# Attention in steps of head pairs: the division of the probabilities moved from VectorE to GpSimd

## What is computed

```python
m = max(scores over all keys, and the sink logit if there is one)
e = exp(scores - m)
p = e / (e.sum(-1) + exp(sink - m))      # the sink's term only where there is a sink
o = p @ v
```

## Time and profile before

| | us |
|---|---|
| median of three runs | 2708.22 |
| lowest and highest | 2704.76, 2711.07 |
| the profiled execution's own time | 2708.02 |
| its span | 2706.2 |
| TensorE busy | 2602.3 |
| VectorE busy | 1407.0 |
| ScalarE busy | 568.7 |
| GpSimd busy | 544.9 |

### The profile page before, as it was taken

How to read it: one execution, slowest core, us unless ns; L and a number is a source line. 1 busy time by engine, 2 the same in 40 slices (tenths; PEclk the granted TensorE clock), 3 DMA queues, 4 the chain that set the end, 5 groups by cost and what they waited for, 6 DMA issues and landing times.

```text
span 2706.2 us, 37981 instructions
## 1 busy us (share of the span) xinstructions
PE 2602.3 (96%) x15358; PEld 1817.8 (67%) x15358; DVE 1407.0 (52%) x2740; ACT 568.7 (21%) x1142; POOL 544.9 (20%) x420
## 2 busy tenths in 40 slices
PE   8999999999999999999999999999999999999998
PEld 4347568888865655789974444788888746555554
DVE  2766376466757677642655653675555427310111
ACT  1216121100033333321022032100000216201110
POOL 0000034344400000038850000354354000000000
PEclk9999999999999999999999999999999999999998
DMA  9540035554333423445436410455543300499995
GB/s 349 199 167 32 31 132 202 179 187 171 114 86 101 116 74 101 141 155 173 156 125 208 142 63 32 151 184 179 172 140 132 111 26 1 195 417 412 416 405 228
DMA packets 222415, 446.67 MB, mean 165 GB/s; under 512 B 18874, under 2 KB 124153, under 8 KB 219163
## 3 DMA queue, kind: packets, MB, share of 16 engines
q1 hardware_dynamic: 180896, 329.78, 34.0%
q10 hardware_dynamic: 41338, 114.40, 12.5%
HBM read 443.01 MB, written 1.13 MB: 164 GB/s over the span
## 4 chain that ended last, share of the span: by engine, by line
PE 88%; DVE 6%; ACT 2%; DMA 1%; issue 1%; POOL 0%; SPq 0%; ACTq 0%; DVEq 0%; POOLq 0%
PE bank L1138 35%; PE bank L966 24%; PE bank L3021 5%; PE bank L990 4%; PE bank L3040 3%; PE bank L982 2%; PE bank_pair L3021 2%; PE bank L559 1%; DMA arena<-in_moe_w 1%; PE bank L2095 1%; PE bank L3057 1%; PE bank_pair L3040 1%; PE bank L2088 1%; PE bank L2994 1%; PE bank L2308 1%
## 5 line engine op out<-in xcount | busy, mean ns | idle before, releaser
L1138 PE MATMUL bank<-arena,slot 128*128 128x256 f32 (+1 forms) x3704 | 677.0, 343 | 6.3 <-DVE arena L1118 2.9
L1138 PEld LDWEIGHTS bank<-arena,slot 128*128 128x128 f32 x3704 | 605.0, 191 | 70.6 <-issue 8.1
L1151 POOL TENSOR_TENSOR slot<-slot 128x512 f32<-128x512 f32 (+3 forms) x208 | 269.2, 1294 | 1556.8 <-PE bank L1138 705.1
L966 PE MATMUL bank<-uT,slot 128*128 128x512 f32 (+2 forms) x1312 | 485.1, 525 | 3.0 <-ACT arena L2128 3.0
L966 PEld LDWEIGHTS bank<-uT,slot 128*128 128x128 f32 (+1 forms) x1312 | 246.8, 190 | 217.3 <-issue 205.0
L1138 PE MATMUL bank<-uT,slot 128*128 128x256 f32 (+1 forms) x1728 | 335.9, 351 | 8.6 <-ACT uT L731 8.3
L1138 PEld LDWEIGHTS bank<-uT,slot 128*128 128x128 f32 x1728 | 291.3, 192 | 46.8 <-ACT uT L731 12.0
L1152 POOL TENSOR_TENSOR slot<-slot 128x512 f32<-128x512 f32 (+3 forms) x208 | 286.5, 1378 | 0.0
L966 PE MATMUL bank<-arena,slot 128*128 128x256 f32 (+1 forms) x576 | 184.5, 483 | 3.4 <-DVE arena L1817 2.3
L966 PEld LDWEIGHTS bank<-arena,slot 128*128 128x128 f32 x576 | 111.4, 194 | 75.0 <-issue 66.3
L700 DVE SCALAR_TENSOR_TENSOR arena<-arena 128x1024 f32<-128x1024 f32 x95 | 122.3, 1297 | 18.2 <-issue 14.5
(11 more groups left out here) (459 smaller groups left out, 2990.3 us busy)
## 6 DMA issues: line engine op xcount, KB each, us to landing
slot<-in_ffn_w SPq DMA_DIRECT2D x42, 2048.0 KB, 8.9
arena<-in_ada_wt ACTq DMA_DIRECT2D x100, 512.0 KB, 3.6
slot<-in_moe_w SPq DMA_DIRECT2D x62, 704.0 KB, 16.5
arena<-in_moe_w SPq DMA_DIRECT2D x52, 704.0 KB, 17.5
rstd<-in_ada_wt ACTq DMA_DIRECT2D x48, 512.0 KB, 3.6
slot<-in_moe_w SPq DMA_DIRECT2D x11, 2048.0 KB, 19.1
slot<-in_ssd_w_in SPq DMA_DIRECT2D x32, 512.0 KB, 6.9
uT<-in_ada_wt ACTq DMA_DIRECT2D x28, 512.0 KB, 3.6
```

The lines of the kernel that those rows point to most:

```text
L966: ins = pe.matmul(bank[0:m, 0:t1 - t0], w[:, k, c0:c0 + m], x[:, k, t0:t1], start=(k == 0), stop=(k == kt - 1))
L1138: ins = pe.matmul(bank[:, u * n:u * n + n], a[:, k, u * P:u * P + P], x[:, k, :], start=(k == 0), stop=(k == self.h - 1))
L1151: pool.tensor_tensor(out[:, :, 0:c], x[:, :, 0:c], y[:, :, 0:c], op)
```

## The change

`Attention` becomes a pooled stage. VectorE computes the reciprocals, raises `shares` and goes on without waiting for them; GpSimd waits for `shares`, does the two multiplications of the unit in place, and raises `divided` after each. TensorE's turn waits for `divided` instead of `pn` where the unit is not a `sub` one.

```diff
         class Attention(Stage):
             all_banks = True
+            pooled = True
...
             def turn(self, pe, B, u, a):
 
-                pe.wait_ge(*S("pn").taken("pe"))
+                pe.wait_ge(*S("pn" if self.units[u]["sub"] else "divided").taken("pe"))
...
                 dve.wait_ge(*S("pr").taken("dve"))
                 if it["sink"] is not None:
                     dve_link(ch, dve.tensor_tensor(den, den, es, ALU.add))
-                dve_link(ch, dve.reciprocal(rc, den))
-                for a in range(2):
-                    s = self.score(u, a)
-                    dve.tensor_scalar(s, s, rc[:, a:a + 1], None, ALU.mult).then_inc(*S("pn").given())
+                dve.reciprocal(rc, den).then_inc(*S("shares").given())
+
+            def pool(self, pool, B, ch):
+
+                for u, it in enumerate(self.units):
+                    if not it["sub"]:
+                        rc = self.stats(u)[4]
+                        pool.wait_ge(*S("shares").taken("pool"))
+                        for a in range(2):
+                            s = self.score(u, a)
+                            pool.tensor_scalar(s, s, rc[:, a:a + 1], None, ALU.mult).then_inc(*S("divided").given())
```

More of the change, by code:

```diff
@@ L285, in build @@
         for n in ("loads", "first_loads", "logit_loads", "mod_ready", "squares", "rstd_used", "root", "normed",
-                  "a_rows", "sg_exp", "gla_d", "gla_e", "gla_q", "gla_sm",                   "gla_s", "gla_sp", "gla_y", "cum_full", "cum_free", "gla_el",                   "conv", "feat", "rows_kept", "seg", "segx", "xw", "st", "padded", "gate_summed", "gated", "lw", "lwx", "ecx",                   "nm", "pr", "pn", "hid", "stored", "dti", "dtx",
+                  "a_rows", "sg_exp", "gla_d", "gla_e", "gla_q", "gla_sm",                   "gla_s", "gla_sp", "gla_y", "cum_full", "cum_free", "gla_el",                   "conv", "feat", "rows_kept", "seg", "segx", "xw", "st", "padded", "gate_summed", "gated", "lw", "lwx", "ecx",                   "nm", "pr", "pn", "shares", "divided", "hid", "stored", "dti", "dtx",
                   "free_a", "bias_loads", "rope_in", "head", "convd", "ada_rows", "ada_cols", "ada_copied", "moe_loads", "da_done", "ready", "lam", "picked", "gate_cols", "overflow_known", "moe_rl", "guest_rows", "token_sums", "weight_sums", "guest_read", "late_const", "hid_done", "tiles_done", "ctx_in", "expert_rows", "ranked", "hid_turned"):
```

## The result

The changed kernel took **2728.86 us** (median of four runs, 2727.95 to 2730.05); the kernel before, run beside it, 2709.38. The ratio is 1.0074, with a 95% interval of 1.0058 to 1.0090: slower by over 0.2%. The forecast was 2713.0 with a range of 2706 to 2722. The measured time lies outside both, and the likeliest case, no change that a measurement can tell, is not what came.

The account below looks back on a forecast made before the run. VectorE was taken to bound both attention patterns by a small margin, TensorE right behind. Even stage +3.1, odd stage +1.2 and TensorE's clock +0.5 made +4.8 us on 2708.22: forecast 2713.0, range 2706 to 2722.

Parts of the forecast that it names:

- the price: GpSimd's time for one division, scaled from its tensor_tensor: 0.90 us for 512 columns, 0.50 for 256.
- the forecast's loops: Repeating chains through two divisions P: even group 9.84 + 2P plus 0.15 port wait, two odd units 5.19 + 2P.
- the dear rival: GpSimd's division as slow as its two-input operation, 1.23 us: near +10, 2718; at 1.5 us, 2724; chance 0.22.
- the forecast's own formulas: Start, loops and end summed per stage: even +0.5, +2.0, +0.6, together +3.1 us; odd +0.5, +0.7, together +1.2.
- three whole loops: Even stage: sixteen units counted as three group loops at about +0.67 us each, +2.0 us.
- the end proper: Even stage's end: the last 256 step's two divisions in the open, 0.22 + 1.00 + 0.10 against 0.7, +0.6 us.
- The start: Each stage's first turn comes 1.22 us behind the reciprocal where it came 0.74 behind: +0.5 us.
- The end lies behind eight sub units and costs nothing: Odd stage's end: no added time, covered by the sub units; without that cover 0.6 us more.
- VectorE bounded by a small margin: Both stages: VectorE sets the pace by 1.4 us of an even group and 0.27 of an odd unit, TensorE right behind.
- the forecast case: Both stages: division of 0.8 to 1.05 us, total +3 to +7 us, 2711 to 2715; chance 0.42.
- The signs named for "wrong": Pitch under 11.1, division far from 0.9, negated maxima of 0.5 us or more, or mid-stage granted clock below 1.00.
- ports or clock: Rival: negated maxima meeting divisions at the shared port, +10 us, or TensorE at half speed inside the pattern, +25; chance 0.10.

Follow-up runs that it names:

- e11_short_both: Against the kernel before: GpSimd divides both heads of the 256-key units only, with the two-input form; 2707.18 us, ratio 0.9995.
- e3_two_inputs: The changed kernel with GpSimd's multiplication by the reciprocal broadcast as a second tensor instead of a scalar; 2712.12 us, ratio 1.0013 to the kernel before.
- e8_no_port: The changed kernel with the negated maximum of units without a sink made in two one-column operations; 2727.34 us, ratio 1.0071 to the kernel before.
- e6_one_head_two_inputs: The changed kernel with VectorE dividing head 0 and GpSimd only head 1, in the two-input form; 2713.98 us, ratio 1.0017 to the kernel before.
- e5_one_head: The changed kernel with VectorE dividing head 0 and GpSimd only head 1, in the scalar form; 2713.23 us, ratio 1.0015 to the kernel before.
- e9_own_first: e6_one_head_two_inputs with GpSimd waiting for VectorE's own division instead of the reciprocal; 2710.24 us, ratio 1.0005 to the kernel before.

## Why the prediction was wrong

**The step that failed is the price.** "I scale the column part by two thirds (0.73 + 0.13 = 0.87) and take 0.90 us." The runs show 1.54 and 0.91, which is 0.28 fixed and 2.5 ns a column: dearer, not cheaper, than the engine's tensor_tensor with two real inputs. One stream less is not one third less. With a broadcast second input the same multiplication takes 1.00, near the 0.90 taken, and with it the forecast's loops hold to 0.1 us. Why the form with a scalar is dearer is open: the pointer is 0.08 of it, the neighbourhood of VectorE none that shows, and the rest was not separated. The Trainium skill ("GPSIMD Engine Reference", "4.1 Engine selection") calls one-input operations of this engine roughly line-rate; this trace differs with 2.5 ns a column for float32 in place, and the measurement decides.

**The bound from above was drawn too low.** The forecast called 1.23 "the only row there is" for the dear rival, noted that more was not excluded and worked out 2724 at 1.5, but let the range end at 2722, and gave all of the dear case 0.22. The nearest row was of another form of instruction; it was read as a ceiling because a simpler operation seemed to have to be cheaper.

**With the true price** the forecast's own formulas give, in the even stage, +1.1 at the start, three times 9.84 + 3.08 + 0.15 - 11.07 = 2.0, and +1.4 at the end: +8.5 of the 13.1 measured. The difference goes both ways:
- *The second loop.* A single pair of divisions was followed. Where GpSimd is dearer than 1.1 us the two 512-key units stand in its queue together: 13.92 a group in place of 13.07, some 0.85 each time.
- *The last group.* "The sixteen units hold three whole loops" left out the fourth group. From unit 12's reciprocal to unit 15's it is 8.75 where it was 5.97: another +2.8. Behind that it is 4.27 where it was 3.14, so the end proper is +1.1, near the +1.4 of the formula. Unit 15's own divisions don't stand in GpSimd's queue. They wait for their reciprocal, and by the chain that waits for ScalarE, which may fill unit 13's buffer only after its late turn (line 2535 is its copy, line 2547 stands behind its exponentials).
- *The start.* Its +1.1 did not come on top. TensorE waits 4.79 for the first division where it waited 3.55, but the first group grew by 2.8, like the third.
- *The clock*, 0.7 us: the second group took 14.60 where the third took 13.92, and it holds the stretch at 0.72. Eight outputs take 0.66 us at the full 2.4 GHz and 1.12 in that stretch. In that group the chain is that of the forecast's loop, two divisions and TensorE's work, stretched by the clock past the 13.92 of the other.

The chain at the end of the even stage, parts left out:

```profile
1645.04 0.60 ACT uT L2535
1645.63 0.95 ACTq L2547
...
1646.61 0.18 DVE small L2593
...
1646.87 1.83 POOL uT L2603 x2
```

In the odd stage the pattern is right: 5.19 + 2 x 1.54 = 8.27 for two units against 8.36 measured, +5.3 over seven units. The start's +1.1 did not come on top here either: the first reciprocal stands 5.5 behind the stage's first matmul in both. "The end lies behind eight sub units and costs nothing" is refuted: 1.85 us came there. From the last unit's reciprocal to the first differential one's it is now 4.21 where it was 2.68, since TensorE's next scores stand behind the turn that waits for the last pair, and VectorE's maxima behind those scores.

```profile
2275.26 0.17 DVE L2593 RECIPROCAL small<-small 128x2 f32<-128x2 f32 x1
2279.47 0.15 DVE L2611 RECIPROCAL small<-small 128x1 f32<-128x1 f32 x1
```

**What was right, and how far.** VectorE bounded by a small margin: taking 4.7 us off VectorE without putting anything on the path bought nothing measurable (e11_short_both). But it was not a queue of VectorE alone. Of the 11.07 us of a group in the kernel before, the way from the turn at 1608.47 to the scores at 1613.92 is TensorE's, and the rest VectorE's; so the division stood in a loop before as well, at VectorE's price. With some 1.3 us less on VectorE in each group (e11_short_both) the group got 0.23 shorter, and the chain of that kernel goes through TensorE for most of it. VectorE's busy time in the even stage fell to 30.0, where 27 was said; the held maxima are 1.6 of the difference (16 of them take 4.3 us, and 2.7 at 0.17). e3_two_inputs is near the forecast case as it was priced: +3.6 us on the medians (ratio 1.0013), where +4.8 was worked out for 0.90. By the stages it is +3.9 and +2.5 (3.4 at a like clock), where the formulas with 1.00 and 0.57 give +4.1 and +1.9. TensorE's waits are released by GpSimd. The signs named for "wrong" were those that came: a division far from 0.9, negated maxima of 0.56 us and a granted clock below 1.00 in the middle of the even stage. Of the rival "ports or clock" the price was wrong: the port's part is hidden (e8_no_port), the clock's is 0.7 in the one group where it can be told, and not 25.

## What to carry to other kernels

Before an operation is moved to an engine that nothing here has seen do it, measure that operation in that form; the price of its neighbour is neither a floor nor a ceiling, and a rewriting of the same arithmetic can change it by a third. When an operation leaves one engine's queue for a hand-over and back, write down every loop that runs through it, with two and with four of it, since queued work on the new engine makes loops that are slack at one price and bind at another. And where two engines share a port, let the one with the short operation go first: a wait added on the other can be a gain (7.70 to about 6.9 for two odd units here). Compare patterns only at the same granted clock: of the 2.14 us by which two of these kernels differ in the even pattern, some 1.6 were the clock and not the port that was being tested.

## What the runs showed of the hardware

- GpSimd, float32 in place on 128 partitions: multiplication by a scalar from memory 1.54 us for 512 columns and 0.91 for 256, by a constant 1.46 and 0.82, by a broadcast tensor 1.00 and 0.57, tensor_tensor with two full inputs 1.23 and 0.68.
- VectorE's division of 128x512 took 1.37 beside a GpSimd operation of 1.04, and 0.49 by itself. A two-column operation of 0.17 was held to 0.56 in the changed kernel and to 1.01 in e3_two_inputs; one-column operations and the maxima from PSUM (0.42 and 0.49) were never seen to grow.
- TensorE's granted clock fell in the middle of the changed even stage. From 1604 to 1612 us, ahead of the stretch at 0.72, TensorE was busy for 6.08 us at a granted clock of 1.00. In the kernel before the clock fell once near the stage's start and then stayed at 1.00. In e6_one_head_two_inputs it fell in each of the two middle groups, in e5_one_head and e9_own_first in neither.

Not tried: a third buffer for the scores, with which GpSimd could work a step ahead, so that its division is in no loop with TensorE.
